# Expert loop of a one-core MoE decoder layer: two weight loads of the next item are put ahead of two loads of the item before

## What is computed

```
logits = xn @ router_w + router_b ; top_val, top_idx = top_k(logits, 4)
gates = softmax(top_val)
# for each expert e, on the tokens that chose it:
gu = xb @ w_gu[e] + b_gu[e]            # w_gu[e]: 1024 x 2048
g, u = gu[:, :1024], gu[:, 1024:]
h = (clip(u, -7, 7) + 1) * (min(g, 7) * sigmoid(1.702 * min(g, 7)))
y = h @ w_down[e] + b_down[e]          # w_down[e]: 1024 x 1024
out[token] += gate * y
```

## Time and profile before

| what | value |
|---|---|
| median of 3 runs | 2252.32 us (2252.26 to 2256.71) |
| the profiled execution: its own time | 2254.76 us |
| its span in the trace | 2253.0 us |
| busy: PE, DVE, ACT, POOL | 2156.8, 1620.0, 1271.3, 453.0 us |
| DMA | 555.98 MB, 247 GB/s over the span |
| granted TensorE clock, mean | 0.983 of full |
| expert loop | from about 732 to 2213 us of the span |

### The profile page before, as it was taken

One profiled execution on the slowest core, in us unless ns is written; L12 is line 12 of the kernel. 1 busy time (PEld: TensorE's weight loads), 2 busy tenths in 40 slices (PEclk: granted clock), 3 DMA queues, 4 the chain that ended last, 5 costly groups with the idle time before them and its releaser, 6 DMA issues.

```text
span 2253.0 us, 32880 instructions
## 1 busy us (share of the span) xinstructions
PE 2156.8 (96%) x9642; PEld 1696.1 (75%) x9643; DVE 1620.0 (72%) x1572; ACT 1271.3 (56%) x1213; POOL 453.0 (20%) x357
## 2 busy tenths in 40 slices
PE   7999999999996899999999999999999999999996
PEld 4454877887685688887887888788878887888873
DVE  5645743405536899787878977997889779997792
ACT  3135342514313577666667756775677567775672
POOL 0792000000000122122231212321322123122210
PEclk9999999999997999999999999999999999999998
DMA  5102232111233799899799979998999799997984
GB/s 174 38 1 93 103 130 88 38 38 38 65 118 130 279 381 377 311 323 312 284 317 362 381 275 319 376 376 315 329 325 373 275 317 377 379 380 274 317 319 168
DMA packets 233717, 555.98 MB, mean 247 GB/s; under 512 B 19972, under 2 KB 20200, under 8 KB 232456
## 3 DMA queue, kind: packets, MB, share of 16 engines
q1 hardware_dynamic: 218448, 512.41, 61.9%
q0 software_dynamic: 13264, 42.63, 7.6%
q10 hardware_dynamic: 1960, 0.35, 0.1%
HBM read 518.38 MB, written 33.69 MB: 245 GB/s over the span
## 4 chain that ended last, share of the span: by engine, by line
PE 80%; issue 8%; DVE 6%; ACT 3%; DVEq 1%; ACTq 1%; DMA 1%; SPq 0%
PE PS L979 21%; PE PS L643 20%; PE PS L983 11%; PE PS L1000 9%; PE PS L1007 5%; PE PS L801 4%; PE PS L841 4%; DVE WL L1934 2%; PE PS L971 2%; PE PS L1032 1%; ACT WH L1339 1%; PE PS L937 1%; PE PS L661 1%; PE PS L1060 1%; ACT WH L1362 1%
## 5 line engine op out<-in xcount | busy, mean ns | idle before, releaser
L1934 DVE TENSOR_TENSOR WL<-WA,WH 128x2048 fp32r<-128x2048 f32 x288 | 651.8, 2286 | 69.7 <-ACT WH L1362 48.8
L1934 DVE TENSOR_TENSOR WL<-H,WH 128x2048 fp32r<-128x2048 f32 x144 | 329.2, 2286 | 79.2 <-ACT WH L1339 58.8
L979 PE MATMUL PS<-WH,XEH 128*128 128x512 f32 x1344 | 362.4, 392 | 2.9 <-DVE WL L1934 2.9
L983 PE MATMUL PS<-WL,XEH 128*128 128x512 f32 x1344 | 353.2, 391 | 0.0
L1362 ACT CAST WH<-WA 128x2048 fp32r<-128x2048 f32 x140 | 267.4, 1911 | 146.1 <-PE PS L1007 145.4
L979 PE MATMUL PS<-WH,XEL 128*128 128x512 f32 x1152 | 311.0, 392 | 0.0
L979 PEld LDWEIGHTS PS<-WH,XEH 128*128 128x128 f32 x1344 | 253.5, 189 | 54.4 <-DVE WL L1934 3.3
L983 PEld LDWEIGHTS PS<-WL,XEH 128*128 128x128 f32 x1344 | 253.7, 189 | 53.1
L979 PEld LDWEIGHTS PS<-WH,XEL 128*128 128x128 f32 x1152 | 218.2, 189 | 46.2
L1000 PE MATMUL PS<-WH,HTH 128*128 128x512 f32 x672 | 187.1, 400 | 4.6 <-DVE HTL L2034 4.6
L1339 ACT CAST WH<-H 128x2048 fp32r<-128x2048 f32 x72 | 136.9, 1910 | 85.4 <-PE PS L983 82.8
(11 more groups left out here) (333 smaller groups left out, 2914.8 us busy)
## 6 DMA issues: line engine op xcount, KB each, us to landing
WA<-in_exp_w_gu SPq DMA_DIRECT2D x216, 1024.0 KB, 7.3
H<-in_exp_w_gu SPq DMA_DIRECT2D x72, 1024.0 KB, 6.4
WA<-in_exp_w_down SPq DMA_DIRECT2D x72, 1024.0 KB, 9.4
H<-in_exp_w_down SPq DMA_DIRECT2D x72, 1024.0 KB, 8.1
WB<-in_xa_wkv SPq DMA_DIRECT2D x4, 2048.0 KB, 7.8
WB<-in_w_in SPq DMA_DIRECT2D x3, 2048.0 KB, 9.1
y_acc<-H SPq DMA_DIRECT2D x9, 512.0 KB, 2.6
H<-in_x SPq DMA_DIRECT2D x4, 1024.0 KB, 5.9
```

The source lines that it names most:

```text
L979: nc.tensor.matmul(PS[:, 2 * h + t, :], x[:, KT4 * half + k, t * P:(t + 1) * P], WH[:, j % 4, k * HALF:(k + 1) * HALF], start=False, stop= ...
L983: ins = nc.tensor.matmul(PS[:, 2 * h + t, :], XEH[:, KT4 * half + k, t * P:(t + 1) * P], WL[:, j % 4, k * HALF:(k + 1) * HALF], start=Fals ...
L1934: v.tensor_tensor(WL[:, s, :], src, WH[:, s, :].bitcast(F32), sub).then_inc(done, 1)
```

## The change

SP's list for an item that has both an item before and a next one becomes: gu6, gu7; dn0, dn1; **gu'0, gu'1**; dn2, dn3; gu'2 to gu'5. Each load keeps the wait that stood before it. Where there is no item before (the first), gu'0 and gu'1 are sent from their old place under a test of `n_p`; where there is no next (the last), the four down pieces go one after another as they did.

```diff
@@ -591,7 +591,15 @@
                 with sp.If_cmp(n_p, 0, "IS_GT"):
                     e_p = entry(sp, 0, i, E - 1)
                     with sp.If_cmp(n_i, 0, "IS_GT"):
-                        for m in range(4):
+                        for m in range(2):
+                            sp.wait_ge(gu_low, 8 * i + m + 3)
+                            load_down(m, bass.ds(e_p, 1))
+                        with sp.If_cmp(n_n, 0, "IS_GT"):
+                            e_n = item_expert(sp, i + 1)
+                            for s in range(2):
+                                sp.wait_ge(gu_low, 8 * i + s + 7)
+                                load_gate_up(s, bass.ds(e_n, 1))
+                        for m in range(2, 4):
                             sp.wait_ge(gu_low, 8 * i + m + 3)
                             load_down(m, bass.ds(e_p, 1))
                     with sp.Else():
@@ -609,13 +617,12 @@
                 with sp.If_cmp(n_n, 0, "IS_GT"):
                     e_n = item_expert(sp, i + 1)
-                    for s in range(6):
-                        if s < 2:
+                    with sp.If_cmp(n_p, 0, "IS_EQ"):
+                        for s in range(2):
                             sp.wait_ge(gu_low, 8 * i + s + 7)
-                        elif s < 4:
-                            sp.wait_ge(dn_low, 4 * i + s + 3)
-                        else:
-                            sp.wait_ge(dn_low, 4 * i + s + 3)
+                            load_gate_up(s, bass.ds(e_n, 1))
+                    for s in range(2, 6):
+                        sp.wait_ge(dn_low, 4 * i + s + 3)
                         load_gate_up(s, bass.ds(e_n, 1))
```

## The result

| | before | changed |
|---|---|---|
| median of 3 runs | 2252.32 us | 2362.64 us (2359.76 to 2365.05) |
| ratio | | 1.0481, 95% interval 1.0467 to 1.0495 |
| span of the profiled execution | 2253.0 us | 2360.9 us |
| busy: PE, DVE, ACT | 2156.8, 1620.0, 1271.3 us | 2194.2, 1617.2, 1269.2 us |
| mean granted clock | 0.983 | 0.972 |

The kernel became 110 us slower. The forecast was 2345, a sum of 90 us, in a range from 2303 to 2382. The added SP code moves each later line of the kernel by 7: L979 is now L986, L937 is L944, L1344 is L1351, L1934 is L1941.

What follows compares the result with a forecast made beforehand. PE was taken as the bound of one-tile items, narrowly ahead of DMA and DVE. Late dn2 in 22 items (42.7 us plain, 20.5 before and 27 second behind two-tile items) summed to 90 us, giving 2345 us, range 2303 to 2382.

Steps and rivals of the forecast that it cites:

- forecast's own case: Whole kernel: dn2 lands about 7.1 us from its issue, time 2330 to 2360 us; chance 0.60.
- Nothing is sent earlier: SP's list: gu'0 and gu'1 go at the same moments as before, held by their waits; only dn2 and dn3 move.
- Step 1, the issue: SP in a one-tile item: dn2 sent 0.64 us behind gu'1, at 1483.5, 9.9 us later than before.
- Step 2, the landing: DMA in a one-tile item: gu'0 takes 5.0 us into the gap, pieces 2.7 us apart, dn2 lands at 1490.6.
- Steps 3 to 5: ACT takes dn2 4.35 us late, DVE's 11.8 us chain gives nothing back, PE waits, next item begins 4.35 us later.
- Where it is hidden: Two-tile items and the six behind them: dn2 1.1 and 4.3 us late, but room or DVE catching up leaves no cost.
- Faster: One-tile items: dn0, dn1 and added rows land sooner, at most 28 us of PE pauses saved, 2226 us; chance 0.03.
- no difference: Loop: dn2 lands before ACT wants it, within 2.7 us of its issue, 2253 us; chance 0.05.
- The smaller sum: 22 one-tile items: by the skill's DMA fit dn2 3.5 us late, sum 71 us, 2326 us; chance of the smaller case 0.15.
- later still: One-tile items: DMA engines catching up delay dn2 a further 1 to 1.5 us, 2365 to 2380 us; chance 0.17, clock included.
- DMA engines' supposed least: Steady one-tile item: transfers of at most about 35.8 us plus new gaps of 2.0 and 0.9 us make 38.7 us.
- The other half of that rival, the clock: PE in 22 items: a tenth of each item's 35 us at 1.2 GHz costs 39 us more, 2384; case's chance 0.17.

Runs made afterwards that it cites:

- e3: Against the kernel before: only gu'0 sent ahead of dn2 and dn3, gu'1 with its wait behind dn3; 2276.25 against 2254.26 us.
- e6: Changed kernel with hidden(1) and the first half of the next tokens ahead of dn2's work on DVE and ACT; 2327.61 us, ratio 1.0324 to the kernel before.
- e2: Against the kernel before: dn2 and dn3 wait for gu7's WL with nothing sent ahead, gu'0 and gu'1 behind them; 2312.03 against 2254.26 us.
- e7: Changed kernel with 5 and 5 unread matmuls on PE ahead of token and hidden transposes in one-tile items; 2356.82 us, ratio 1.044 to the kernel before.
- e11: Changed kernel with 8 and 8 unread matmuls on PE in one-tile items; 2359.39 us, the changed kernel again on the same chip 2363.69 us.
- e5: Changed kernel with gu'2 too sent ahead of dn2 and dn3; 2443.99 us against 2255.02 us for the kernel before.
- e8: Kernel before with hidden(1) ahead of dn2's WL on DVE, SP's list the old one; 2269.13 against 2255.02 us.

## Why the prediction was right

2362.64 us lies in the range, but not in the forecast's own case (2330 to 2360): it is 2.6 us above it. The mechanism was right and the sum 18 us too small.

*What bounds the kernel* was read right: no slack but dn2's 4.0 us. *Nothing is sent earlier*: gu'0 goes 13.4 us after the item's start in both kernels (1975.26 less 1961.9; 1479.24 less 1465.89).

*Step 1, the issue*: 0.62 us behind gu'1, forecast 0.64. *Step 2, the landing*: from gu'0's issue to dn2's landing 11.3 us, forecast 1490.6 less 1479.24, 11.4; a piece sent into the gap took 5.0 to 5.1 us. The rows of a two-tile item, where the queue does run empty, and the rate of a full queue were the right sources. *Steps 3 to 5*: ACT 4.4 us late (forecast 4.35), DVE's chain from the start of dn2's WL to the end of the last tokens 11.83 us (11.84 before), then transposes with 0.97 us idle and 0.63 us of issue before L978, as in the one item of before that already waited. *Where it is hidden*: the two-tile items and the ones behind them.

*The rivals.* Faster and no difference didn't come: dn2 needed 7.0 us from its issue, not 2.7. The smaller sum from the 4.4 us of the Trainium skill's fit (DMA: Bandwidth & Descriptors, section Anatomy of one DMA) didn't come either; the page gives that fit for DMAs issued from GpSimd, and these are issued from SP; the trace has 5.0 us alone and about 2.5 between two. Of "later still" a part came. Gaps of the DMA engines were not the cause: e3 and e6 have items shorter than the DMA engines' supposed least, and in e2 the items are longer by dn2's lateness and no more (late pieces ahead of it add to that lateness in the five items before a two-tile one). The other half of that rival, the clock, was the cause of most of it, but of about 12 us where it had priced 39.

*The term that was too small* is the clock: I took it at 1.00 for the sum, since the stretch of 39.0 us had kept it. That was a selective reading, for the trace of the kernel before has the opposite case too. Its items of 37.1 and 37.7 us, and the paused one ahead of the second:

```profile
770.03:807.13 37.10, 37.10 (x165) 30.58 (x165) 32.91 (x23) 25.20 (x19) 6.33 (x5) 0.96 1.04 393
...
1147.00:1185.70 38.70, 36.56 (x167) 29.18 (x164) 32.71 (x23) 30.65 (x23) 12.19 (x7) 1.00 0.92 310
1185.70:1223.40 37.70, 37.27 (x164) 30.61 (x164) 33.56 (x23) 25.79 (x19) 9.47 (x6) 0.95 1.01 364
```

An item with 2.1 us of PE pauses is followed by one with the clock at 0.95. And I had taken these two long items to hold some pause that would soak up part of dn2's delay; the first has none (37.10 of 37.10 us busy), the second 0.4 us. They were long by the clock.

In the changed kernel some items run partly at 1.2 GHz. The first 10 us of the item of 41.5 us, and its rest:

```profile
1517.10:1527.10 10.00, 9.96 (x37) 8.06 (x38) 7.45 (x6) 5.25 (x5) 3.14 (x1) 0.83 1.05 380
1527.10:1558.60 31.50, 28.04 (x129) 22.36 (x127) 25.52 (x18) 21.70 (x16) 7.78 (x6) 1.00 0.88 314
```

Right behind the pauses at the end of the item before, the clock is at half for part of the time, and this item is 1.6 us longer than its neighbours of 39.9. The way from clock to time leads over dn2 again. In the item of the same kind that starts at 2001.8, SP sends dn2 and ACT takes it at:

```profile
2020.98 0.99 SPq L556 DMA_DIRECT2D H<-in_exp_w_down  x2
...
2028.15 1.91 ACT L1351 CAST WH<-H 128x2048 fp32r<-128x2048 f32 x1 [4.49 <-DMA H<-in_exp_w_down]
```

That is 19.2 and 26.35 us after the start, where the item before it has 17.6 and 24.8: gate/up at half clock holds back the WL of gu6 and gu7, and with it what SP sends behind their waits. By the items' lengths against their kind's, such stretches account for about 12 of the 18 us that the forecast lacked (five one-tile items with 1.4 to 2.2 us each, and two two-tile items of 54.9 us with 1.4). For three of them e7 and e11 show it by taking it away; for the others it is read from the clock alone. The Trainium skill (TensorE: Matmul & The Clock Gate, Part 1) says that the array's clock follows how busy PE has been, between half and full; the trace agrees, with the clock at 0.83 there behind pauses like those shown above (1.61, 0.26, 0.97 and 0.63 us), and back at 1.00 with the pauses filled. The remaining 6 us are one item in which dn2 took 8.1 us to land and not 7.0, and a few that were already longer than 35.5 us before, for which I had taken off up to 1.8 us too much (that one is the item of 37.1 us above). Why the clock falls behind one item's pauses and not behind another's of the same length stays open.

## What to carry to other kernels

A list of DMA issues with semaphore waits is served in order: moving a load ahead of another gains only if its own wait is met sooner than the old place is reached, and each load behind it inherits its wait and its bytes. Before such a swap, work out for the passed load when it would be sent (the wait ahead), when it would land (idle latency, or the spacing of a full queue), and how much slack it has; past that slack each microsecond came back one for one in the changed kernel, e2, e3 and e5, where the engines behind it work in order without room. In e5 the two-tile items paid too. Read the granted clock item by item before putting it at 1.00: a row of before showed what its mean over the loop hid. Where a piece must come late, put the work that doesn't need it ahead of it on the in-order engines (e6), and don't do so where it comes in time (e8).

## What the runs showed of the hardware that I hadn't expected

Transfers of 1 MB into emptied queues took 5.0 us, and a full queue gave one each 2.5 to 2.7 us. In e2, with all pieces late, the gap of the DMA engines was 1.7 us an item where 5.5 were worked out. Pauses of PE that add up to 3.5 us in an item of 39.9 us brought the mean granted clock of the loop from 1.00 to 0.98; in e5, with 4.5 us of pauses in a steady item, it was 0.95. An item with the clock at 0.83 over its first 10 us lost 1.6 us, since its loads went out later; another lasted 44.4 us with the clock at 0.92 and at 1.00, with 4.5 and 6.5 us of pauses.
